# RWKV-7 layer of a diffusion step: each pair's preparation takes one value projection unit between its two gates, and pairs are inverted one by one

## What is computed

```python
r, k, v = heads(xr @ w_r), heads(xk @ w_k), heads(xv @ w_v)
kk = k * k_k; kk = kk * rsqrt(sum(kk * kk) + 1e-12)          # per head
for dirn in range(2):
    decay = exp(-exp(-softplus(-(w0 + tanh(xw @ w_l1) @ w_l2)) - 0.5))
    a = sigmoid(a0 + (xa @ a_l1) @ a_l2)
    k_eff = k * (1 + (a - 1) * k_a)
    # scan: sa = s @ -kk; s = s * w + sa (kk * a)^T + v k_eff^T; y = s @ r
    bonus = sum(r * k_eff * r_k) * v
```

## Time and profile before

| | us |
|---|---|
| median of 3 runs (3582.57 to 3597.68) | 3586.53 |
| the profiled execution | 3597.06 |
| its span | 3595.3 |
| granted PE clock over the span | 0.965 |
| PE, DVE, ACT, POOL busy | 3289.7, 1824.1, 1283.5, 1450.1 |
| last key unit ends, value units start | 1569.4 |
| last pair prepared | 1800.6 |
| first and last pair scanned | 1859.1, 2186.4 |

### The profile page before, as it was taken

One profiled execution on the slowest core, in us unless ns is written; L12 is line 12 of the kernel. 1 busy time (PEld: TensorE's weight loads), 2 busy tenths in 40 slices (PEclk: granted clock), 3 DMA queues, 4 the chain that ended last, 5 costly groups with the idle time before them and its releaser, 6 DMA issues.

```text
span 3595.3 us, 74626 instructions
## 1 busy us (share of the span) xinstructions
PE 3289.7 (92%) x29474; PEld 3044.0 (85%) x29474; DVE 1824.1 (51%) x3105; ACT 1283.5 (36%) x2116; POOL 1450.1 (40%) x716
## 2 busy tenths in 40 slices
PE   5899999999999998897477889999998999999998
PEld 2689999899899997795277778899997877899997
DVE  7743765564437545938933443436545644421113
ACT  3343223422432235437422333432234233532223
POOL 0355334554553334432765103553334301563334
PEclk9999999999999999997589999999999999999999
DMA  7544554433445443346454432445443200342223
GB/s 271 168 119 151 193 188 151 124 112 101 119 144 204 146 144 107 123 138 210 153 155 113 116 80 76 128 147 204 146 141 112 91 7 18 124 135 82 71 76 119
DMA packets 208608, 468.08 MB, mean 130 GB/s; under 512 B 88810, under 2 KB 98602, under 8 KB 206890
## 3 DMA queue, kind: packets, MB, share of 16 engines
q1 hardware_dynamic: 179850, 445.12, 39.2%
q10 hardware_dynamic: 28512, 19.45, 1.7%
HBM read 423.44 MB, written 41.06 MB: 129 GB/s over the span
## 4 chain that ended last, share of the span: by engine, by line
issue 74%; POOL 18%; POOLq 7%; PE 1%; DVE 0%; DMA 0%; ACT 0%; DVEq 0%; SPq 0%
POOL ws L759 17%; POOLq L792 3%; POOLq L789 3%; PE banks L867 1%; POOLq L767 1%; POOLq L794 0%; PE banks L877 0%; POOLq L758 0%; POOLq L780 0%; DVE banks L2468 0%; DMA wr<-in_w_slabs 0%; POOLq L759 0%; PE banks L896 0%; PE banks L912 0%; DVE x L2473 0%
## 5 line engine op out<-in xcount | busy, mean ns | idle before, releaser
L759 POOL TENSOR_TENSOR ws<-wr,ws 128x1024 fp32r<-128x1024 f32 x509 | 1237.9, 2432 | 1975.3 <-ACT ws L1704 1974.7
L1704 ACT ACTIVATE ws<-wr 128x1024 fp32r<-128x1024 f32 x509 | 537.9, 1057 | 1053.9 <-PE banks L851 441.3
L846 PE MATMUL banks<-hs,ws 128*128 128x320 f32 x3712 | 564.3, 309 | 0.3 <-DVE hs L2852 0.2
L846 PEld LDWEIGHTS banks<-hs,ws 128*128 128x128 f32 x3712 | 549.3, 188 | 1.1 <-DVE hs L2852 0.8
L867 PE MATMUL banks<-hs,ws 128*128 128x320 f32 (+2 forms) x2624 | 441.8, 318 | 40.4 <-DVE hs L2490 14.1
L867 PEld LDWEIGHTS banks<-hs,ws 128*128 128x128 f32 x2624 | 400.8, 192 | 68.4 <-issue 24.6
L867 PE MATMUL banks<-fs,ws 128*128 128x320 f32 x2304 | 374.2, 312 | 13.8 <-DVE fs L3235 7.7
L2631 DVE SCALAR_TENSOR_TENSOR mjunk<-mr,banks 128x1024 f32<-128x1024 f32 x284 | 335.5, 1219 | 75.1 <-DMA mr<-in_m_slabs 51.2
L867 PEld LDWEIGHTS banks<-fs,ws 128*128 128x128 f32 x2304 | 344.0, 188 | 32.1 <-issue 12.6
L846 PE MATMUL banks<-fs,ws 128*128 128x320 f32 x2304 | 350.9, 310 | 0.0
L846 PEld LDWEIGHTS banks<-fs,ws 128*128 128x128 f32 x2304 | 341.5, 188 | 2.3 <-issue 2.3
(11 more groups left out here) (317 smaller groups left out, 4023.2 us busy)
## 6 DMA issues: line engine op xcount, KB each, us to landing
wr<-in_w_slabs SPq DMA_DIRECT2D x509, 512.0 KB, 3.6
mr<-in_m_slabs SPq DMA_DIRECT2D x167, 512.0 KB, 5.0
ar_d<-ar SPq DMA_DIRECT2D x16, 640.0 KB, 3.3
bk_d<-bt SPq DMA_DIRECT2D x16, 640.0 KB, 6.1
bk<-bk_d SPq DMA_DIRECT2D x16, 640.0 KB, 4.3
ar<-ar_d SPq DMA_DIRECT2D x32, 320.0 KB, 4.4
mx<-in_m_slabs SPq DMA_DIRECT2D x16, 512.0 KB, 6.5
rkv<-rkv_d SPq DMA_DIRECT2D x24, 320.0 KB, 5.1
```

Of the source, the lines that this page charges most:

```text
L759: pool.tensor_tensor(ws[s % 2][:, 1, :], wr[:, s % 2, :], ws[s % 2][:, 0, :].bitcast(F32), ALU.subtract).then_inc(lo_ready, 1)
L846: pe.matmul(pu[:, t % 2, h, 0:HT], ws[s % 2][:, 0, k * P:(k + 1) * P], src[:, k, part, h * HT:(h + 1) * HT], start=(k + part == 0), stop=F ...
L1704: act.activation(ws[s % 2][:, 0, :], wr[:, s % 2, :], ACT.Copy).then_inc(hi_ready, 1)
```

## The change

- Value unit 0 is issued in three parts among pair 0's first steps; unit m + 1 stands in pair m's turn of the loop, whole, between the decay and rate gates of pair m + 1. All units use one half of `pu` (VT), the gates the other half and `aux[:, 2:4]`, the banks of the diagonal products. The values go to DVE from `relu`, not through a load.
- Squares and sums of all eight pairs' key norms stand among the key units; one root, one reciprocal serve all.
- Each pair is inverted by itself, 80 partitions, one pair's elements per partition. Pair 0's inversion is cut in three, a weight slab's low part after each. SP stores each inverse after the scan before it ends.
- The last two multiplications of a direction are one. The products of window ends are made in each scan. Outputs 3 to 6 are rounded after the last scan. The bonus product comes after direction 0 for pair 0 too.

The buffers that move with this (`blocks`, `inv_a`, `inv_x`, `inv_t`, `rr`) are not shown.

```diff
...
-rkv = place("rkv", [P, 2, 3, T])
+rkv = place("rkv", [P, 2, 2, T])
...
-def gates_at(m):
-    return (pu[:, 0], pu[:, 1]) if m >= 2 else (aux[:, 0:2], aux[:, 2:4])
+def gates_at():
+    return pu[:, 1 - VT], aux[:, 2:4]
...
+        load_until(at[0] + 1)
         for m in range(KD):
-            if m == 3:
-                load_blocks(0, 2)
+            if m + 1 < KD:
+                load_until(at[0] + 1)
...
                 load_receptance(m + 2)
-                load_values(m + 2)
-            if m == KD - 1:
+            if m == 1:
+                load_blocks(0)
+            if m == KD - 3:
...
         load_inputs(0, 1)
-        load_blocks(1, KD)
+        sp.wait_ge(aab_done, 2 * KD)
+        load_blocks(1)
+        load_blocks(2)
...
             sp.wait_ge(y_done, m + 1)
-            if m == 1:
-                store_inverses(1)
-                load_blocks(2, KD)
-            if m == 3:
-                store_inverses(2)
+            store_inverses(m + 1)
             for d in range(2):
                 load_inverted(m + 1, d)
+            if m + 3 < KD:
+                load_blocks(m + 3)
...
-    def invert(i):
-        m0, m1, q = INV_PAIRS[i]
-        n = 16 * NW * (m1 - m0) // q
-        x, t, blocks_in = inv_x[i][0:n, 0:q, :, :], inv_t[i][0:n, :], inv_a[i][0:n, 0:q, :, :]
-        pool.wait_ge(inv_landed, 16 * (i + 1))
...
+    def identities(i):
+        x = inverted(i)[0]
+        pool.wait_ge(inv_landed[i % 2], 16 * (i // 2 + 1))
...
+    def eliminate(i, j0, j1):
+        x, blocks_in, t = inverted(i)
+        for j in range(j0, j1):
             r = 31 - j
-            tj = t[:, 0:q * r * (j + 1)].rearrange("p (q r c) -> p q r c", q=q, r=r)
-            shape = [n, q, r, j + 1]
-            pool.tensor_tensor(tj, blocks_in[:, :, j + 1:32, j:j + 1].to_broadcast(shape),
-                               x[:, :, j:j + 1, 0:j + 1].to_broadcast(shape), ALU.mult)
+            tj = t[:, 0:r * (j + 1)].rearrange("p (r c) -> p r c", r=r)
+            shape = [16 * NW, r, j + 1]
+            pool.tensor_tensor(tj, blocks_in[:, j + 1:32, j:j + 1].to_broadcast(shape),
+                               x[:, j:j + 1, 0:j + 1].to_broadcast(shape), ALU.mult)
             pool.drain()
-            rows = x[:, :, j + 1:32, 0:j + 1]
+            rows = x[:, j + 1:32, 0:j + 1]
             pool.tensor_tensor(rows, rows, tj, ALU.add)
             pool.drain()
-        pool.tensor_copy(blocks_in, x.rearrange("p q r c -> p q c r")).then_inc(inv_pool, 1)
...
+        x, blocks_in, _ = inverted(i)
+        pool.tensor_copy(blocks_in, x.rearrange("p r c -> p c r")).then_inc(inv_pool, 1)
...
-    low_parts(0, taken)
-    invert(0)
+    low_parts(0, taken - 4)
+    identities(0)
+    for n, (j0, j1) in enumerate(((0, 10), (10, 20), (20, 31))):
+        eliminate(0, j0, j1)
+        if n == 2:
+            transposed(0)
+        low_part(taken - 4 + n)
+    low_part(taken - 1)
     pool.wait_ge(prep_ready, 2 * KD)
+    for stored in rkv_stored:
+        pool.wait_ge(stored, 16 * 2 * KD)
...
-    for i in range(1, 3):
-        invert(i)
+    for i in range(1, KD):
+        identities(i)
+        eliminate(i, 0, 31)
+        transposed(i)
     low_parts(taken, n_slabs)
...
-        units(hs, KD // 2, mix_ready["k"], 0)
-        lora_unit(mix_ready["g"], lambda k: fs_raw[:, k // 2, k % 2, :])
-        units(hs, KD // 2)
-        def value_units(n):
-            for _ in range(n):
+        def key_unit(m):
...
+        def key_sums(m):
+            pe.wait_ge(kksq_ready, m + 1)
+            for w in range(NW):
+                mm = pe.matmul(st[:, 1, SN * m + 2 * w:SN * m + 2 * w + 2], ksq[m % 2][:, w * P:(w + 1) * P],
+                               blk[:, 0:P:HS], start=True, stop=True, skip_group_check=True)
+            mm.then_inc(kksq_summed, 1)
+        pe.wait_ge(rwkv_landed, 48)
+        for m in range(KD):
+            if m == KD // 2:
+                lora_unit(mix_ready["g"], lambda k: fs_raw[:, k // 2, k % 2, :])
+            key_unit(m)
+            if m:
+                key_sums(m - 1)
+        def value_part(part):
+            s, t = slab[0], tile[0]
+            if part == 0:
...
+                pe.wait_ge(hi_ready, s + 1)
+                pe.wait_ge(tile_read, t if t > rwkv_tiles - KD else t - 1)
+            if part == 2:
+                pe.wait_ge(lo_ready, s + 1)
+                for k in range(KD):
+                    for h in range(2):
+                        mm = pe.matmul(pu[:, VT, h, 0:HT], ws[s % 2][:, 1, k * P:(k + 1) * P],
+                                       fs[:, k, 0, h * HT:(h + 1) * HT], start=False, stop=(k == KD - 1))
+                mm.then_inc(tile_done, 1)
                 slab[0] += 1
                 tile[0] += 1
+                return
+            for k in range(4 * part, 4 * part + 4):
+                for c in range(2):
+                    for h in range(2):
+                        pe.matmul(pu[:, VT, h, 0:HT], ws[s % 2][:, 0, k * P:(k + 1) * P],
+                                  fs[:, k, c, h * HT:(h + 1) * HT], start=(k + c == 0), stop=False)
...
-            gate_products(m, 0, tw)
...
-            pe.wait_ge(kksq_ready, m + 1)
-            if m == 1:
...
+            if d == 0 and m + 1 < KD:
+                pe.wait_ge(b1_th, 2 * m + 4)
...
-        value_units(1)
-        pe.wait_ge(lora_ready, 1)
-        pe.wait_ge(rwkv_landed, 16)
-        key_sums(0)
+        value_part(0)
+        key_sums(KD - 1)
         decay_gates(0)
-        value_units(2)
+        value_part(1)
         rate_gates(0)
-        value_units(2)
+        value_part(2)
         spread(0)
-        value_units(1)
...
-        diagonal(0, 1)
-        pe.wait_ge(tile_read, tile[0])
-        for m in range(1, KD):
+        for m in range(KD):
+            if m:
+                diagonal(m - 1, 1)
             if m + 1 < KD:
-                key_sums(m + 1)
                 decay_gates(m + 1)
+                for part in range(3):
+                    value_part(part)
+                rate_gates(m + 1)
             bonus(m)
-            if m + 1 < KD:
-                rate_gates(m + 1)
             diagonal(m, 0)
             if m + 1 < KD:
                 spread(m + 1)
-            diagonal(m, 1)
+        diagonal(KD - 1, 1)
+        pe.wait_ge(tile_read, tile[0])
         pe.wait_ge(b1_done, KD)
+        pe.wait_ge(blk_ready, 2 * KD)
...
+        def key_squares(m):
+            if m >= 2:
+                act.wait_ge(kksq_summed, m - 1)
+            act.activation(ksq[m % 2], relu[:, m % 2, :], ACT.Square, scale=pv[:, 4, m:m + 1]).then_inc(kksq_ready, 1)
...
             ahead()
             store_tile(t + 2 + m + (m >= KD // 2), m, 1, 2 * KD + m)
+            key_squares(m)
...
-            store_tile(t + m, m, 2, 3 * KD + m)
-        def key_squares(m):
-            act.wait_ge(k_landed[m % 2], 32 * (m // 2 + 1))
...
+            n = 3 * KD + m
+            act.wait_ge(tile_done, t + m + 1)
+            act.wait_ge(rkv_stored[n % 2], 16 * (n // 2))
+            if m >= 2:
+                act.wait_ge(b1_done, m - 1)
+            act.activation(halves(relu[:, n % 2, :]), pu[:, VT, :, 0:HT], ACT.Copy).then_inc(tile_read, 1)
+            act.wait_ge(tile_read, t + m + 1)
+            act.dma_start(rkv_d[m, 2], relu[:, n % 2, :]).then_inc(rkv_stored[n % 2], 16)
...
-            key_roots(m)
...
+        value_high(0)
         act.wait_ge(lw_zeroed, 1)
-        value_high(0)
-        key_squares(0)
+        act.wait_ge(kksq_summed, KD)
+        act.activation(roots, st[:, 1, 0:KD * SN], ACT.Sqrt, bias=eps_kk[:, :]).then_inc(kk_root, 1)
+        decays(0)
+        rates(0)
+        value_high(1)
         value_store(0)
-        value_high(1)
...
-        slab[0], tile[0] = s + KD, t + KD
-        take_blocks(0, 0)
-        for m in range(1, KD):
-            if m + 1 < KD:
-                key_squares(m + 1)
+        for m in range(KD):
             exponents(m, 0)
-            take_blocks(m - 1, 1)
+            if m:
+                take_blocks(m - 1, 1)
             exponents(m, 1)
             if m + 1 < KD:
                 decays(m + 1)
                 rates(m + 1)
+                value_store(m + 1)
+                if m + 2 < KD:
+                    value_high(m + 2)
             take_blocks(m, 0)
+        slab[0], tile[0] = s + KD, t + KD
         take_blocks(KD - 1, 1)
...
-            dve.wait_ge(k_landed[j], 32 * (m // 2 + 1))
...
-                dve.tensor_tensor(by_window(bt[j][d][:, 0, :]), by_window(bt[j][d][:, 0, :]), e_n, ALU.mult)
-                dve.tensor_tensor(by_window(bt[j][d][:, 1, :]), by_window(bt[j][d][:, 1, :]), e_n, ALU.mult
+                both = bt[j][d][:, :, :].rearrange("p c (w n) -> p c w n", w=SN)
+                dve.tensor_tensor(both, both, e_n.unsqueeze(1).to_broadcast([P, 2, SN, SW]), ALU.mult
                                   ).then_inc(prep_ready, 1)
-                if d == (m == 0):
-                    if m + 1 < KD:
```

(65 more changed lines are left out.)

149 lines of the change are left out of this document (47 added, 102 removed).

## The result

The changed kernel takes 3545.7 us in the median (3544.64 to 3559.69), the kernel before 3587.7 beside it: a ratio of 0.9889, 95% interval 0.9856 to 0.9921. The forecast was 3541.5, the range 3518 to 3570. The profiled execution took 3544.64 (span 3542.9, granted clock 0.972), where the one before took 3597.06.

What follows compares the result with a forecast made beforehand. The preparation was taken as two stages waiting on each other's engine, PE then DVE. Interleaving gains 34 us, the scans 11; 45 off the profiled 3597.06 gives 3552, from the median 3541.5, range 3518 to 3570.

Steps and rivals of the forecast that it cites:

- Key phase, +8.3: Key units on PE: seven key-norm sums now stand between them at 1.2 us each, adding 8.3 us.
- K: Start of the first value part on PE, forecast at 1569.4 + 8.3 = 1577.7 us.
- Lead-in, K + 35: Start of the preparation: pair 2's decay gates come 35 us after the first value part starts.
- Five rings, 5 x 22.8 + 5: Preparation's pair loop: five turns of a PE and ACT wait cycle, 19.8 us plus 3 for clock, plus 5 for POOL contention.
- Clock, 3 us a pair: PE in the preparation: idling before each decay gate makes following work start throttled, costing 3 us a pair.
- POOL beside DVE, 18 of which 5 stay: Preparation: pair 0's inversion costs DVE half of 35.5, 18 us; DVE's slack leaves about 5 us.
- The fourth rival: Preparation: DVE is shut out for all of POOL's 46 us inversion, 28 us more, 3569.5; chance 0.10.
- DVE 19.3 a pair: Preparation: DVE's own need is 17.1 us a pair plus 2.2 us beside POOL's low part, 19.3.
- End of the preparation, E = 1766: End of DVE's pair 7 forecast at 1766 us, where it was 1800.6: 34 us gained.
- Scans: After the preparation: single-pair inversions take 45.5 us each, the end comes 375 us after preparation, 11 us gained.
- POOL sets them by 7: Scans: POOL's inversions end them 375 us after the preparation, the scans alone 368, so POOL sets it by 7.
- Sum: Whole kernel: 34 us from the preparation and 11 from the scans, 45 us gained.

Runs made afterwards that it cites:

- the run with both edits: Changed kernel with ACT's value high part between decays and rates, and PE's rate gates and bonus sum moved ahead within the value unit: 3542.42 us, ratio 0.986.
- the run without the inversion: Changed kernel with pair 0's elimination on POOL left out, its memset, copy, transfers and low parts kept: 3540.09 us, ratio 0.9852.
- the run with five columns less: Changed kernel with 5 of 31 elimination columns left out in each of the seven inversions between the scans: 3542.0 us, ratio 0.9877.
- the second profile: Profile of the unaltered changed kernel run once more, as measure for three runs beside it on the same chip: 3546.39 us, ratio 0.986.

## Why the prediction was right

**Key phase, +8.3.** Nearly right: one sum beside a unit costs 1.03 us, seven of them 7.2, and the phase grew by 7.9. K came at 1574.99 and not 1577.7, as the first key unit began 2.3 us earlier in this execution (1501.09 and not 1503.44).

**Lead-in, K + 35.** The decay gates of pair 2 start at 1609.86, K + 34.9.

**Five rings, 5 x 22.8 + 5.** 119 predicted, 116.2 measured (1609.86 to 1726.05). The size was right, the ring was not. I had drawn it through ACT alone, "that never passes DVE", with 19.8 us of operations and 3 of clock. What stands in the trace is first scan, e_in, exponents, blocks, decay gates (5.0 us), unit, rate gates, bonus (13.8), four DVE operations (3.8), next first scan: 22.6. It passes DVE. A ring through ACT nearly as long seems to be there too: with the bonus alone moved the period is 23.4 to 23.9. Both hold the unit and are nearly of one length, and that is luck: the sum came out by it. The failed step would have misled anyone who used it: by it, moving the rate gates forward saves 12 to 15 us, and that run's median was 13 higher, its P by 5 and 9, for the most part through pair 0.

**Clock, 3 us a pair.** 2.75 measured: 1.15 in the decay gates and 1.6 in the unit's first 32 matmuls. The rule on oscillation that I cited from the Trainium skill ("TensorE: Matmul & The Clock Gate", HAM oscillation) holds here: the decay gates of pairs 2 to 7 started at half clock. In one pair of the run with both edits the slow stretch came later: pair 3's decay gates took 1.35 us behind a wait of 1.63, and the 16 matmuls behind them 4.14 us and not 2.6.

**POOL beside DVE, 18 of which 5 stay.** DVE lost 9.6, and 5.6 to 9.3 stayed in P. The half of 35.5 us was too high. The fourth rival, that DVE stands still for each of POOL's microseconds, falls by the run without the inversion. The Trainium skill's rule of an exclusive lock ("SBUF — State Buffer", Who interferes with whom) is not settled by that, since by it the one that comes second waits, which can be POOL. POOL did wait: the same inversion kept it busy 64.6 us here and 36.0 beside a scan. For single low parts the traces agree with the rule: four DVE operations of 0.8 to 1.5 us took 1.9 to 2.2 longer beside one.

**DVE 19.3 a pair.** Right: in the run with both edits, 19.14 and 19.35 in the two pairs where nothing else holds it.

**End of the preparation, E = 1766.** 1759.95: 2.7 of the difference is K, 2.8 the rings, the rest the tail (33.9 us from the last decay gates, 34.5 predicted).

**Scans.** First inversion at E + 13.8 (15), one inversion 45.2 (45.5), the last scan's end at E + 370 (375), the first scan's at E + 48.2 (53; in the twelve other profiles it is 3 to 7 us later, so this one was short). From the last inverse to its scan's end 40.2 where I took 41.5. "POOL sets them by 7": 7 by the run with five columns less. I expected waits of a few us at the xd matmuls in every pair, and this step failed: only scan 1 has them (2.21 and 2.95 us; 0.7 in scans 1 and 2 of the second profile), and in the others all loads of the inverse are in time. So the size is shown, and the way is not. The inverses' stores and loads take about 4 us until the first load is issued (1863.92 to 1867.87) and not the 4.9 that I kept of 9.9.

**Sum.** 34 + 11 = 45 predicted; 40.7 + 15.7 = 56.4 measured up to the last scan between two single executions, 42 between the medians. The execution profiled before stood 10.5 us above its median, as said; the remainder is within the spread of both.

## What to carry to other kernels

When a ring of waits is summed from a profile, follow it by what releases what, since a wrong ring of the right length predicts the total and misleads every edit. Before reordering one engine, look where the background work of a sharing engine will fall: here the 2.1 us of one low part, on e_in or ahead of the bonus, decided whether the same order on PE gained nothing or 6 us. Look at the first turn by itself: moving the rate gates alone lost 6.4 us there. A wait of TensorE costs more than its length when the work behind it starts at half clock: here 2.75 us a pair on top.
